# Attention's read-outs and weight lows in another order, and cross attention's prompt chain ahead of its last decode scores

## The reference, cut to what matters

```python
m = mixer(x)                      # differential attention | state space part, then @ w_out
x = layer_norm(ALPHA * x + m)
x = layer_norm(ALPHA * x + cross_attention(x))
x = layer_norm(ALPHA * x + channel(x))   # layer 0: dense gated product, layer 1: 8 experts
```

```python
s = einsum('bqhd,bkhd->bhqk', q, mem_k) * MEM_HEAD_DIM ** -0.5
o = einsum('bhqk,bkhd->bqhd', softmax(s), mem_v)
return o.reshape(b, L, D_MODEL) @ w_co
```

## Time and profile before

| | us |
|---|---|
| median of 3 runs (1751.18 to 1751.96) | 1751.26 |
| the profiled execution, its own time | 1749.58 |
| its span, from the first to the last instruction | 1747.6 |
| PE busy (share of the span) | 1690.4 (97%) |
| DVE busy | 1214.2 (69%) |
| ACT busy | 847.1 (48%) |
| POOL busy | 193.6 (11%) |

### The profile page before, as it was taken

The page is one execution under the profiler, slowest core; times in us unless marked ns, Lnnn a source line. Parts: engine busy times, 40 slices in busy tenths (PEclk is TensorE's granted clock), DMA queues, the critical chain, the costliest instruction groups (busy, mean ns, idle before and its releaser), DMA issues.

```text
span 1747.6 us, 23355 instructions
## 1 busy us (share of the span) xinstructions
PE 1690.4 (97%) x8729; PEld 1325.6 (76%) x8729; DVE 1214.2 (69%) x1558; ACT 847.1 (48%) x890; POOL 193.6 (11%) x149
## 2 busy tenths in 40 slices
PE   7999999899999999999989999999999999999997
PEld 4655487699999665548768888888888888888885
DVE  2687554655553358755463698888988989899987
ACT  1122331344443112233132577777777777777774
POOL 0540100200000054010022300000000000000001
PEclk9999999999999999999999899999999999999999
DMA  9656543775534446654276598999999999999993
GB/s 321 202 206 218 216 171 119 262 226 193 181 133 145 149 154 209 217 217 180 115 269 240 181 359 310 390 374 386 384 375 387 377 394 372 391 372 392 372 394 118
DMA packets 220580, 466.23 MB, mean 267 GB/s; under 512 B 11134, under 2 KB 50232, under 8 KB 220486
## 3 DMA queue, kind: packets, MB, share of 16 engines
q1 hardware_dynamic: 213446, 444.76, 70.1%
q0 software_dynamic: 4752, 16.25, 3.2%
q10 hardware_dynamic: 2304, 4.20, 0.6%
HBM read 447.10 MB, written 18.21 MB: 266 GB/s over the span
## 4 chain that ended last, share of the span: by engine, by line
PE 88%; DVE 7%; ACT 2%; issue 1%; DMA 1%; SPq 0%; ACTq 0%; DVEq 0%
PE bank L1291 85%; PE bank L1295 3%; DVE arena L2819 1%; DMA out<-mem_rows 1%; DVE arena L2718 1%; DVE R L2418 0%; ACT arena L1932 0%; DVE arena L2933 0%; DVE st L2791 0%; DVE st L2697 0%; DMA ring<-in_x_sample 0%; ACT SQ L1953 0%; DVE pair_in L2437 0%; ACT xT L1968 0%; DVE arena L2799 0%
## 5 line engine op out<-in xcount | busy, mean ns | idle before, releaser
L2283 DVE TENSOR_TENSOR ring_low<-ring,high 128x2048 fp32r<-128x2048 f32 x264 | 600.8, 2290 | 81.8 <-ACT high L1867 81.3
L1867 ACT ACTIVATE high<-ring 128x2048 fp32r<-128x2048 f32 x264 | 506.6, 1919 | 150.2 <-PE bank L1291 142.7
L1291 PE MATMUL bank<-high,xg_high 128*128 128x512 f32 x704 | 278.0, 395 | 0.0
L1291 PE MATMUL bank<-ring_low,xg_high 128*128 128x512 f32 x704 | 275.0, 391 | 0.0
L1291 PE MATMUL bank<-high,xg_low 128*128 128x512 f32 x704 | 274.7, 390 | 0.0
L1291 PEld LDWEIGHTS bank<-ring_low,xg_high 128*128 128x128 f32 x704 | 132.5, 188 | 28.2
L1291 PEld LDWEIGHTS bank<-high,xg_high 128*128 128x128 f32 x704 | 132.6, 188 | 27.2
L1291 PEld LDWEIGHTS bank<-high,xg_low 128*128 128x128 f32 x704 | 132.8, 189 | 26.4
L1291 PE MATMUL bank<-high,he_high 128*128 128x512 f32 x352 | 139.1, 395 | 0.0
L1932 ACT ACTIVATE arena<-bank 128x512 f32<-128x512 f32 (+3 forms) x89 | 43.7, 522 | 194.3 <-PE bank L1291 142.2
L1291 PE MATMUL bank<-ring_low,he_high 128*128 128x512 f32 x352 | 137.2, 390 | 0.0
(11 more groups left out here) (348 smaller groups left out, 2750.0 us busy)
## 6 DMA issues: line engine op xcount, KB each, us to landing
ring<-in_w_exp_gu SPq DMA_DIRECT2D x176, 1024.0 KB, 14.0
ring<-in_w_exp_down SPq DMA_DIRECT2D x40, 2048.0 KB, 16.1
ring<-in_w_in SPq DMA_DIRECT2D x12, 2048.0 KB, 11.2
ring<-in_w_ffn_gu SPq DMA_DIRECT2D x22, 1024.0 KB, 8.0
ring<-in_w_ckv SPq DMA_DIRECT2D x8, 2048.0 KB, 8.4
ring<-in_cache_mem_k SPq DMA_DIRECT2D x16, 1024.0 KB, 8.1
ring<-in_cache_mem_v SPq DMA_DIRECT2D x16, 1024.0 KB, 6.9
ring<-in_cache_attn_k SPq DMA_DIRECT2D x32, 256.0 KB, 4.2
```

The lines of the kernel that those rows point to most:

```text
L1291: return M.matmul(out, lhsT, rhs, start=start, stop=stop)
L1867: S.activation(high_bufs[h % HIGH_BUFS][:], ring[:, s, j * HALF:(j + 1) * HALF], ACT.Copy).then_inc(split_high, 1)
L2283: V.tensor_tensor(ring_low[:, s, part], ring[:, s, part], high_bufs[h % HIGH_BUFS][:], ALU.subtract).then_inc(split_low, 1)
```

## The change

In self attention ACT makes high 1 of `w_out` ahead of `aT` (in another place of the arena, on the tile of turned keys and queries), and memory part 6 behind the second `rms`; part 7 and highs 2 and 3 come behind all of `mixT`. DVE makes lows 0 and 1 of `w_out`, behind `rms(0)`, and POOL no longer does. PE does the first five eighths of memory part 7 ahead of the last two `mixT` and the rest behind them. `mem_k` and `mem_v` change places in the arena, and SP loads `mem_k` after four stores and the last `rms`.

In cross attention PE does both `cS` of a tile before it spreads the second half of the query rows, ACT instead of DVE scales the probabilities (DVE only takes the reciprocals), and the turned probabilities and the first two `cO` stand ahead of `sCT`. The warm-up matmuls ahead of `cPT` are two for each tile instead of eleven for the second. ACT's exp for the decode row stands ahead of the last `oT_high`.

```diff
@@ PsumTurns
-    def __init__(self, groups, banks, full, emptied):
+    def __init__(self, groups, banks, full, emptied, emptied_behind=()):
...
+        order = [g for g, _ in groups]
+        for name, other in emptied_behind:
+            order.remove(name)
+            order.insert(order.index(other) + 1, name)
...
+    def ahead(self, pe, name):
+        n = self.index[name]
+        by = self.groups[n - len(self.banks)][1]
+        pe.wait_ge(self.emptied[by], self.rank[n - len(self.banks)])
         return self.banks[n % len(self.banks)]
@@ psum_groups
         for n in MIX_ORDER:
-            if n == 2:
-                add("A", "mkv", 7)
             add("V", "mixT", n)
+        add("A", "mkv", 7)
...
-        for n in range(4):
-            add("A", "cS", n // 2, n % 2)
-            if n == 0:
+        for t in range(2):
+            add("A", "cS", t, 0)
+            if t == 0:
                 add("V", "qsT", 1)
-            add("V", "qsb", 2 * n, 1)
-            add("V", "qsb", 2 * n + 1, 1)
+            add("A", "cS", t, 1)
+            add("V", "qsb", 2 * t, 1)
+            add("V", "qsb", 2 * t + 1, 1)
         for t in range(2):
             for kt in range(2):
                 add("A", "cPT", t, kt)
+            if t == 0:
+                for b in range(4, 8):
+                    add("V", "qsb", b, 1)
+        add("V", "cO", 0)
+        add("V", "cO", 1)
         add("V", "sCT")
-        for i in range(4):
-            add("V", "cO", i)
+        add("V", "cO", 2)
+        add("V", "cO", 3)
@@ arena
-        out_high = [parts_in(f"out_high{h}", "arena", at, [HALF]) for h, at in enumerate((6208, 9216, 4160, 0))]
+        out_high = [parts_in(f"out_high{h}", "arena", at, [HALF]) for h, at in enumerate((6208, share, 4160, 0))]
...
-        mem_v = carve(2 * 1024).rearrange("p (t n) -> p t n", t=2)
-        mem_k = carve(2 * 1024, share).rearrange("p (t n) -> p t n", t=2)
+        mem_k = carve(2 * 1024).rearrange("p (t n) -> p t n", t=2)
+        mem_v = carve(2 * 1024, share).rearrange("p (t n) -> p t n", t=2)
@@ turns = PsumTurns(...)
+                          [((l, "mkv", 6), (l, "aT", 1, 1)) for l in range(L)])
@@ SP
-                sp.wait_ge(mem_stored, 16 * 8 * (l + 1))
+                sp.wait_ge(mem_stored, 16 * (8 * l + 4))
                 passed(sp, (l, "O", 1))
+                mix_ready.wait(sp, l, NORM_ORDER.index(1))
...
                 copied(sp, (l, "m", 0))
+                sp.wait_ge(mem_stored, 16 * 8 * (l + 1))
@@ POOL
-                for j in range(2):
-                    out_high_ready.wait(pool, l, j)
-                    raw, low = half_of((l, "out", 0), j)
-                    G.tensor_tensor(low, raw, out_high[j][:], ALU.subtract).then_inc(out_low_by_pool.sem, 1)
@@ PE, self attention
+                def memory_products(bk, i, ks):
                     c, t = divmod(i, 2)
                     w = slot((l, "ckv", c)).rearrange("p (k n) -> p k n", k=KT)
+                    for k in ks:
+                        last = mm(bk[:], memT[:, k, t * P:(t + 1) * P], w[:, k, :], k == 0, k == KT - 1)
+                    return last
...
                 for n in MIX_ORDER:
                     if n == 2:
-                        memory_part(7)
+                        memory_products(turns.ahead(pe, (l, "mkv", 7)), 7, range(5))
...
+                full(memory_products(turns.open(pe, (l, "mkv", 7)), 7, range(5, KT)))
@@ PE, cross attention
+                def turned(t):
                     for kt in range(2):
                         bk = turns.open(pe, (l, "cPT", t, kt))
-                        if t and not kt:
-                            warm(bk, 11)
+                        if not kt:
+                            warm(bk, 2)
                         cP_ready.wait(pe, l, t)
...
+                for t in range(2):
+                    scores(t, 0)
+                    if t == 0:
+                        q_rows(1)
+                    scores(t, 1)
+                    for b in (2 * t, 2 * t + 1):
+                        q_on_all(b, 1)
+                turned(0)
+                for b in range(4, 8):
+                    q_on_all(b, 1)
+                turned(1)
+                copied(pe, (l, "cPT", 1, 1))
+                pe.wait_ge(mem_v_landed, 16 * (l + 1))
+                values(0)
+                values(1)
+                bk = turns.open(pe, (l, "sCT"))
+                last_scores.wait(pe, l, 2)
+                copied(pe, (l, "qsb", 7, 1))
...
+                values(2)
+                values(3)
@@ ACT, self attention
                 weights_high("out", 0, out_high, out_high_ready)
                 memory_part(5)
-                memory_part(6)
+                weights_high("out", 1, out_high, out_high_ready)
                 take_aT(1, 0)
                 take_aT(1, 1)
                 rms(1)
-                weights_high("out", 1, out_high, out_high_ready)
+                memory_part(6)
                 rms(2)
                 for n in MIX_ORDER:
-                    if n == 2:
-                        weights_high("out", 2, out_high, out_high_ready)
-                        memory_part(7)
...
-                weights_high("out", 3, out_high, out_high_ready)
+                memory_part(7)
+                for h in (2, 3):
+                    weights_high("out", h, out_high, out_high_ready)
@@ ACT, cross attention
+                def normalize(t):
+                    cr_ready.wait(act, l, t)
+                    for h in range(MH):
+                        ins = S.activation(cP[:, t, h, :], cP[:, t, h, :], ACT.Copy, scale=rr[:, 4 * t + h:4 * t + h + 1])
...
+                cross_exps(0)
+                normalize(0)
+                cross_exps(1)
+                take_turned(0)
+                normalize(1)
+                take_turned(1)
+                for i in range(3):
+                    attended_high(i)
                 cs_rows.wait(act, l)
...
+                attended_high(3)
@@ DVE, self attention
                 rms(0)
+                for h in (0, 1):
+                    weights_low("out", h, out_high, out_high_ready, out_low_ready)
                 bk = take(dve, (l, "oS"))
@@ DVE, cross attention
-                def normalize(t):
+                def reciprocals(t):
                     copied(dve, (l, "cS", t, 1))
-                    step.done(V.reciprocal(rr[:, 4 * t:4 * t + 4], rs[:, 4 * t:4 * t + 4]))
-                    for h in range(MH):
-                        ins = V.tensor_scalar(cP[:, t, h, :], cP[:, t, h, :], rr[:, 4 * t + h:4 * t + h + 1], None,
-                                              ALU.mult)
...
+                    V.reciprocal(rr[:, 4 * t:4 * t + 4], rs[:, 4 * t:4 * t + 4]).then_inc(cr_ready.sem, 1)
...
-                for n in range(4):
-                    row_maxima(n)
-                    if n == 0:
-                        take_q_rows(1)
-                    if n == 2:
-                        normalize(0)
-                    for b in (2 * n, 2 * n + 1):
-                        if b == 7:
-                            normalize(1)
-                        memory_scores(b, 1)
+                row_maxima(0)
+                take_q_rows(1)
+                row_maxima(1)
+                for b in (0, 1):
+                    memory_scores(b, 1)
+                reciprocals(0)
+                row_maxima(2)
+                row_maxima(3)
+                memory_scores(2, 1)
+                reciprocals(1)
+                for b in range(3, 8):
+                    memory_scores(b, 1)
+                attended_low(0)
+                attended_low(1)
                 dve.wait_ge(dve_steps, step.n)
                 bk = take(dve, (l, "sCT"))
...
-                for i in range(3):
-                    attended_low(i)
+                attended_low(2)
```

More of the change, by code:

```diff
@@ L152, in __init__ @@
         seen = {k: 0 for k in emptied}
-        self.rank = []
-        for _, by in groups:
+        order = [g for g, _ in groups]
+        for name, other in emptied_behind:
+            order.remove(name)
+            order.insert(order.index(other) + 1, name)
+        self.rank = [0] * len(groups)
+        for g in order:
+            by = groups[self.index[g]][1]
             seen[by] += 1
-            self.rank.append(seen[by])
+            self.rank[self.index[g]] = seen[by]
         self.opened = 0
@@ L1347, in block_of, with columns_of @@
                 full(last)
-            def columns_of(l, name, i, bufs, low_ready, xh, xl, ready=None):
+            def columns_of(l, name, i, bufs, low_ready, first, xh, xl, ready=None):
                 s = rg.arrived(pe, (l, name, i))
@@ L1360, in columns_of @@
                         if m == 0 and k % 4 == 0:
-                            low_ready.wait(pe, l, k // 4)
+                            low_ready.wait(pe, l, first + k // 4)
                         if ready and m == 0:
@@ L1444, in memory_part @@
                         copied(pe, ("mem", 3))
-                    for k in range(KT):
```

(37 more changed lines are left out.)

44 lines of the change are left out of this document (20 added, 24 removed).

## The result

The changed kernel took 1729.07 us in the median of 6 runs (1726.64 to 1736.22) beside 1751.22 for the kernel before (6 runs): a ratio of 0.9884, 95% interval 0.9864 to 0.9905. In two later measurements, on chips 3 and 7, it was 1728.62 (0.9862, 0.9845 to 0.9880) and 1729.78 (0.9878, 0.9858 to 0.9898). Faster was right, since all three intervals lie under 1; the time lies 6.8 us under the predicted 1735.9 and under the range's lower end, 1732.

The account below looks back on a forecast made before the run. It took TensorE's chain of waits to bound the kernel, at the end of self attention and in cross attention; 7.0 + 8.4 = 15.4 off 1749.58 gave 1734.2, or 1735.9 us on the median's scale, range 1732 to 1744.5.

Parts of the forecast that it names:

- The two lows ... and its new wait: End of attention, layer 0: DVE takes two lows from POOL, 2.28 us each; PE then idles 2.5 before oSt at 210.2.
- Out starts at 226.8: 4.0 earlier: End of attention, layer 0: PE starts the out product at 226.8 instead of 230.79; layer 1 gains 3.0 us.
- 0.8 off each: End of attention: 0.8 us taken off each layer's gain for a possible low clock spell after the new idle before oSt.
- 1.6 for the second spell: Layer 0's out product: the slow clock after another idle stretch should go, counted as 1.6 us gained.
- The term of 7.0: End of attention, both layers: 3.2 + 2.2 + 1.6 for the second spell = 7.0 us, between 4.0 and 8.7.
- 4.2 earlier in each layer: Cross attention: weighted values (oV) begin at 329.0 instead of 333.24, 8.4 us in all; range 2.6 to 4.6 per layer.
- DVE's last score ... + 1.2 + 0.6: Cross attention: DVE's last score at 322.5, from 323.07 less 2.3 for scalings plus 1.2 and 0.6 lost in waits.
- co's weights ... hidden, with 1.4 to spare: Cross attention: co's weights, loaded from near 319, are ready in time; second low at 339.7, needed at 341.1.
- the first rival: End of cross attention: co's weights become the bound; with cross attention's gain lost altogether, 1744.3 us; chance 10%.
- Slower by the clock: Rival, cross attention: with seven warm-ups fewer PE falls to the 1.2 GHz level until oV ends, 1766.7 us; chance 7%.
- The gain does not reach the end: Rival: the later expert phase is set by its weight stream, not PE, so time stays at 1751 us; chance 7%.
- On the median's scale: Whole kernel: the profiled execution's 1749.58 less 15.4 gives 1734.2 us, restated as 1735.9 since the median is 1.7 higher.

## Why the prediction missed

The way in which the gain comes about was right in the main; two terms of the sum were mis-sized. Cross attention, put at 4.2 a layer, measured 5.6: a wait of DVE was counted as lost that a row maximum fills, and the tail up to oV was priced too long. The end of attention, put at 7.0, measured 9.3: O(1) was priced at the low clock, which it never had, and 0.8 a layer for a slow spell was taken off on top. The landmarks give 20.4 where the sum had 15.4; the interval of the ratio leaves 16.6 to 23.8. The other 2 of the 22 us gained by the median are within that interval; the old kernel's slow out in layer 1, which the prediction put in layer 0 alone, may hold some of them, which was not settled.

- **"The two lows ... and its new wait"**: right. oSt came at 210.16 in the old frame (210.44 - 0.28) for 210.2, PE's idle was 2.47 for 2.5, the second tile was ready at 221.8 for 221.8.
- **"Out starts at 226.8: 4.0 earlier"**: 0.7 short. O(1) took 1.95, not the slow 3.53 that I had priced, so part 7 began 0.7 sooner.
- **"0.8 off each" for a clock spell**: a spell costs 0.8 (24.8 against 24.0) and is paid at fifteen of twenty places, but on other work than I had priced. It makes oSt, the turning and the warm-ups behind it slow, so that O(1) starts 12.9 instead of 11.3 behind rms; O(1) itself takes 1.95 to 2.00 at all twenty. Layer 1 of the profile, with the spell:

```profile
767.98 1.21 PE L1308 MATMUL bank<-arena,const 128*8 128x512 f32 x2 [2.47 <-DVE arena L2807]
769.12 1.97 PE L1312 MATMUL bank<-const,arena 128*128 128x128 f32 x8
...
772.78 1.95 PE L1308 MATMUL bank<-arena 128*128 128x128 f32 x16
```

The base of 4.0 and 3.0 had one spell in it already, in O(1), and it is what comes where both layers pay one: 4.0 (28.76 - 24.8) and 3.0. Taking off 0.8 counted it twice, 3.2 and 2.2 against 4.7 and 3.0 in the profile. "1.6 for the second spell" measured 1.50. The term of 7.0 should have been 8.5 with a spell in both layers; it was 9.3 with one.

- **What the attention part's gain is made of**: I gave ACT's wait for the store a share of its own (O(1) 1.2 earlier). With POOL's lows back and all else new, O(1) began 8.8 behind rms instead of 12.1 (211.10 - 202.32, 214.17 - 202.03), yet out came no earlier: POOL's hold moved to the square of the decode rows. So while POOL makes the lows, the new orders of ACT, PE and SP gain nothing by themselves; the 4.7 come when DVE doesn't meet POOL, 1.8 as a hold and 2.9 as the slow clock behind it. What DVE's lows would gain with ACT's old order was not run.
- **"4.2 earlier in each layer"**: 5.6 measured; this is the larger of the two terms that failed, 2.8 of the 5.0 by which the sum fell short. "DVE's last score ... + 1.2 + 0.6" counted a wait as lost that a row maximum moved ahead of it fills (0.82), and DVE ended at 321.4 (315.43 and the 5.96 by which cS is earlier) instead of 322.5. PE's two cO then end last, at 321.75, so that 0.8 of this counted; the tail from the transpose to oV was 5.85 for 6.45. I put no lower bound on the 1.2, so the upper end of my range for a layer, 4.6, lay under what came.
- **"co's weights ... hidden, with 1.4 to spare"**: right in layer 0. In layer 1 the load took 11.7 instead of 9.8, and the first rival came true in small: a wait of up to 1.3, in some profiles alone, and up to 2.3 with the slow clock.
- **"Slower by the clock"**: it didn't happen, since the four warm-ups left hold the clock at 1.00; without them it costs 2.6 and 3.9.
- **"The gain does not reach the end"**: it did; from experts to the end of the span it was 768.7 and 769.3.
- **"On the median's scale"**: the profiled execution, 1734.08, hit the 1734.2 of the sum by chance: terms 5 too small, and 4.3 given back behind co. Its own time lay 5 us above its kernel's median, where that of before lay 1.7 below.

## What to carry to other kernels

A wait of TensorE can be paid twice: with its length, and with the slow matmuls behind it. Here that came behind 15 of 20 waits of 2.5 us. Price both, once, on the matmuls that stand right behind the wait, and ask of each order what keeps PE at work through it. When an instruction is moved ahead of a wait, take it off the work behind it before the wait is counted as lost. Where run times scatter by more than a term is worth, compare stretches between fixed instructions of two profiles, which here mostly repeat to 0.05 us where the clock is the same.

## What the runs showed of the hardware

- POOL's 128x2048 subtraction held a DVE operation on only eight partitions until 1.07 us behind its own end: 5.47 instead of 1.22.
- The same wait of 2.5 us at the same instruction was followed by a slow spell (granted clock 0.77 over 7.5 us) at fifteen places and by none at five; it cost 0.8 each time.
- At 20 to 40 us the mean granted clock was 0.66, 0.83 or 0.91 in runs of nearly the same program, and all that followed moved by up to 4.7 us (rms at 200.64, 202.31 and 205.38).
